# The front of a hybrid decoder block: constants, first row tiles, first weight slab and row loads in another order

## The reference

```python
h = rmsnorm(x, g_mix[l])
proj = h @ w_in[l]          # 1024 x 4000
c_q, c_kv, k_rope_raw, bcx, gate_logits = jnp.split(
    proj, [COL_CQ, COL_CKV, COL_KROPE, COL_CONV], axis=-1)
attn = mla_attention(c_q, c_kv, k_rope_raw, cos, sin, g_cq[l], w_uq[l], g_ckv[l], w_ukv[l])
conv = gated_short_conv(bcx, conv_w[l])
gates = jax.nn.sigmoid((gate_logits + b_gate[l]).astype(jnp.float32)).astype(x.dtype)
mixed = g_a * (attn @ w_branch_a[l]) + g_b * (conv @ w_branch_b[l])
x = x + mixed @ w_out[l]
```

## Time and profile before

| | us |
|---|---|
| median of 3 runs | 2920.02 |
| lowest and highest | 2916.92, 2920.36 |
| the profiled execution | 2914.94 |
| its span in the profile | 2913.1 |
| PE busy in it | 2670.8 (92%) |
| DVE busy | 1669.3 (57%) |
| ACT busy | 1387.2 (48%) |
| POOL busy | 665.4 (23%) |

### The profile page before, as it was taken

One profiled execution on the slowest core, in us unless ns is written; L12 is line 12 of the kernel. 1 busy time (PEld: TensorE's weight loads), 2 busy tenths in 40 slices (PEclk: granted clock), 3 DMA queues, 4 the chain that ended last, 5 costly groups with the idle time before them and its releaser, 6 DMA issues. The chain is left out here.

```text
span 2913.1 us, 37842 instructions
## 1 busy us (share of the span) xinstructions
PE 2670.8 (92%) x12830; PEld 2083.5 (72%) x12830; DVE 1669.3 (57%) x2262; ACT 1387.2 (48%) x2316; POOL 665.4 (23%) x708
## 2 busy tenths in 40 slices
PE   6999999999998999999799999899967999999980
PEld 5777787787775666666689898677656777777760
DVE  3623624524426666655554453465566888888858
ACT  4334334324323666667611112543416777777853
POOL 0000000000003555555322220000003444444420
PEclk9999999999998999999899999999978999999995
DMA  4253353354442112212345344232267999999978
GB/s 167 83 189 130 109 171 115 124 171 169 131 134 48 37 39 55 47 37 75 108 131 150 112 134 160 84 109 102 77 255 267 370 373 374 374 383 387 374 279 353
DMA packets 168851, 508.67 MB, mean 175 GB/s; under 512 B 40448, under 2 KB 69760, under 8 KB 140576
## 3 DMA queue, kind: packets, MB, share of 16 engines
q1 hardware_dynamic: 150016, 472.56, 47.4%
q0 software_dynamic: 18720, 34.64, 3.2%
HBM read 432.21 MB, written 108.33 MB: 186 GB/s over the span
## 5 line engine op out<-in xcount | busy, mean ns | idle before, releaser
L487 DVE TENSOR_TENSOR fr_wl<-fr_raw,fr_wh 128x1024 fp32r<-128x1024 f32 x128 | 156.8, 1225 | 470.5 <-ACT fr_wh L358 470.2
L358 ACT CAST fr_wh<-fr_raw 128x1024 fp32r<-128x1024 f32 x128 | 134.0, 1047 | 493.0 <-PE fr_acc L282 493.0
L2547 DVE TENSOR_TENSOR ex_gl<-ba_raw,ex_gh 128x2048 fp32r<-128x2048 f32 x128 | 293.2, 2292 | 101.8 <-ACT ex_gh L2460 101.8
L2460 ACT CAST ex_gh<-ba_raw 128x2048 fp32r<-128x2048 f32 x128 | 245.2, 1917 | 39.5 <-PEq L2055 39.5
L909 ACT ACTIVATE at_pf<-at_psS 128x512 f32<-128x512 f32 (+1 forms) x320 | 178.3, 558 | 167.1 <-PE at_psS L794 84.2
L1027 POOL TENSOR_TENSOR at_pl<-at_pf,at_ph 128x512 fp32r<-128x512 f32 (+1 forms) x160 | 195.4, 1221 | 258.7 <-ACT at_ph L910 258.2
L983 DVE TENSOR_TENSOR at_pl<-at_pf,at_ph 128x512 fp32r<-128x512 f32 (+2 forms) x160 | 145.7, 914 | 139.7 <-ACT at_ph L910 136.5
L944 DVE TENSOR_REDUCE at_nm<-at_psA 128x1 f32<-128x512 f32 (+2 forms) x320 | 183.0, 605 | 63.2 <-PE at_psA L828 43.1
L2397 PE MATMUL ex_psG<-ex_gh,ex_xh 128*128 128x512 f32 x512 | 200.7, 392 | 6.7 <-DVE ex_xl L2552 5.3
L2398 PE MATMUL ex_psG<-ex_gl,ex_xh 128*128 128x512 f32 x512 | 200.3, 391 | 0.0
L2399 PE MATMUL ex_psG<-ex_gh,ex_xl 128*128 128x512 f32 x512 | 200.1, 391 | 0.0
(11 more groups left out here) (367 smaller groups left out, 6469.7 us busy)
## 6 DMA issues: line engine op xcount, KB each, us to landing
ba_raw<-in_w_exp SPq DMA_DIRECT2D x192, 1024.0 KB, 19.0
fr_raw<-in_w_slabs SPq DMA_DIRECT2D x128, 512.0 KB, 3.8
gates_d<-fr_gst SPq DMA_DIRECT2D x64, 256.0 KB, 4.3
mx_gt<-gates_d SPq DMA_DIRECT2D x64, 256.0 KB, 5.3
cb_ys<-y_d SPq DMA_DIRECT2D x16, 1024.0 KB, 10.9
mx_xr<-in_x SPq DMA_DIRECT2D x8, 1024.0 KB, 7.1
x_d<-mx_xo SPq DMA_DIRECT2D x8, 1024.0 KB, 5.0
xa_xe<-x_d SPq DMA_DIRECT2D x16, 512.0 KB, 5.5
```

The costliest lines, as they stand in the source:

```text
L487: V.tensor_tensor(wl[:, i % 2], raw[:, i % 2], wh[:, i % 2], ALU.subtract).then_inc(w_lo, 1)
L2460: nc.scalar.copy(gh[:, s, i], raw[:, r, i, :].rearrange("p (k n) -> p k n", k=KD // 2)).then_inc(w_hi, 1)
L2547: V.tensor_tensor(gl[:, s, i], raw[:, r, i, :].rearrange("p (k n) -> p k n", k=KD // 2), gh[:, s, i], ALU.subtract).then_inc(w_lo, 1)
```

## The change: what it does

1. **Constants.** The block for `cst`, `vec` and `masks` is gone. Their three loads are issued in the front's SP queue, after tile 1 and ahead of slab 0. PE waits for them ahead of the first turn, ACT and DVE after their part of the start.
2. **Table.** ACT computes one square root of one column (of `eps`) before it waits for tile 0.
3. **Banks.** Tiles 1 and 2 are turned into `psL` 0, 1 and 2, 3; tile 3 goes into `tp` again and waits for tile 0 alone. ACT splits tile 3 ahead of casting slab 1, and DVE splits tiles 2, 3 in another order about the first `low`.
4. **First slab.** Its first eight matmuls wait for the four `hh` and for `wh`, the next eight for `wl`, the last for `hl`.
5. **PE kept busy.** 14 products of `ones` by `ones` (128 x 128, 32-bit) ahead of the first turn, four after each of the four turns. Their result is not used.
6. **Rows.** The first two tiles of quarters 2 and 3, and the two tiles of mem, are issued at n = 26 and 27 of the quarter before the one in which they are turned (that is, 5 or 6 slabs ahead of where they were). The first two tiles of quarter 1 are still issued at n = 0 and 1 of quarter 0. The others stay at n = 4 and 6.

```diff
-                pe.wait_ge(out_lo, ti)
+                if ti >= 4:
+                    pe.wait_ge(out_lo, ti)
+                elif ti == 3:
+                    pe.wait_ge(out_lo, 1)
...
+            for dst, src in zip((cst, vec, masks), consts):
+                sp.dma_start(dst[:], src).then_inc(c_in, 16)
...
-                    if more and n in (0, 1, 4, 6):
-                        rows(TQ * (q + 1) + (0, 1, 4, 6).index(n))
-                    if not more and n < MT:
-                        rows(NT + n)
+                    if q == 0 and n < 2:
+                        rows(TQ + n)
+                    if more and n in (4, 6):
+                        rows(TQ * (q + 1) + n // 2)
+                    if more and n in (26, 27):
+                        rows(TQ * (q + 2) + n - 26)
...
+                if i == 0:
+                    pe.wait_ge(out_hi, 2 * TQ)
+                    pe.wait_ge(w_hi, 1)
...
+                    if i == 0 and j == 1:
+                        pe.wait_ge(w_lo, 1)
+                    if i == 0 and j == 2:
+                        pe.wait_ge(out_lo, TQ)
...
+            pe.wait_ge(ones_set, 1)
+            keep_busy(14)
+            pe.wait_ge(c_in, 48)
             for ti in range(TQ):
                 turn(ti)
+                keep_busy(4)
...
+            nc.scalar.activation(st[:, 3, 1:2], eps[:], ACT.Sqrt)
...
-        with nc.Block() as block:
-            @block.sync
-            def _(sp):
-                sp.dma_start(cst[:], a["consts"]).then_inc(c_in, 16)
-                sp.dma_start(vec[:], a["vecs"]).then_inc(c_in, 16)
-                sp.dma_start(masks[:], a["masks"]).then_inc(c_in, 16)
-                sp.wait_ge(c_in, 48)
```

More of the change, by code:

```diff
@@ L100, in front @@
 def front(nc, cst, vec, x, g_mix, w_slabs, pos, w_uq, w_uk, w_uv, gates_d, conv_d, qn_d, qr_d, kn_d, kr_d, v_d,
-          mem, g_mem, w_kv, hh0, hl0, wk_mem, wv_mem, memT, kv_in):
+          mem, g_mem, w_kv, hh0, hl0, wk_mem, wv_mem, memT, kv_in, masks, consts, c_in):
     QS = 1.0 / math.sqrt(QKD)
@@ L171, in x_landed, with turn_space @@
             return (x_in[ti], 16) if ti < 4 else (x_in[ti % 2], 16 * (2 + (ti - 4) // 2))
+        def turn_space(ti, half):
+            if ti in (1, 2):
+                return psL[2 * (ti - 1) + half][:].rearrange("p (k n) -> p k n", k=4)
+            return tp[half][:]
         def angle_count(q):
@@ L264, in turn, with keep_busy @@
                 pe.wait_ge(norm_done, ti + 1)
-                pe.wait_ge(out_lo, ti)
+                if ti >= 4:
+                    pe.wait_ge(out_lo, ti)
+                elif ti == 3:
+                    pe.wait_ge(out_lo, 1)
                 for k in range(KD):
-                    mm = nc.tensor.transpose(tp[k // 4][:, k % 4, :], xn[:, ti % 2, k * P:(k + 1) * P], ident)
+                    mm = nc.tensor.transpose(turn_space(ti, k // 4)[:, k % 4, :], xn[:, ti % 2, k * P:(k + 1) * P], ident)
                 mm.then_inc(turned, 1)
+            def keep_busy(n):
+                for _ in range(n):
+                    nc.tensor.matmul(acc[1][:, 0:P], ones[:], ones[:], start=True, stop=True)
             def slab(q, n):
                 i = N * q + n
-                if n == 0:
-                    pe.wait_ge(out_lo, TQ * (q + 1))
-                pe.wait_ge(w_lo, i + 1)
+                if i == 0:
+                    pe.wait_ge(out_hi, 2 * TQ)
+                    pe.wait_ge(w_hi, 1)
+                else:
+                    if n == 0:
+                        pe.wait_ge(out_lo, TQ * (q + 1))
+                    pe.wait_ge(w_lo, i + 1)
                 if i >= 2:
@@ L403, in split_out @@
                 for half in (1, 0):
-                    nc.scalar.copy(hh[Q % 2][:, 4 * half:4 * half + 4, tile], tp[half][:]).then_inc(out_hi, 1)
+                    nc.scalar.copy(hh[Q % 2][:, 4 * half:4 * half + 4, tile], turn_space(ti, half)).then_inc(out_hi, 1)
             def memory_out(m):
@@ L450, in _ @@
             split_out(2)
+            split_out(3)
             high(1)
-            split_out(3)
+            act.wait_ge(c_in, 48)
             for q in range(NC_):
@@ L504, in split_out @@
                     f = slice(4 * half, 4 * half + 4)
-                    ins = V.tensor_tensor(hl[Q % 2][:, f, tile], tp[half][:], hh[Q % 2][:, f, tile], ALU.subtract)
+                    ins = V.tensor_tensor(hl[Q % 2][:, f, tile], turn_space(ti, half), hh[Q % 2][:, f, tile], ALU.subtract)
                 ins.then_inc(out_lo, 1)
@@ L602, in _ @@
             norm(3)
+            split_out(2)
             low(0)
-            split_out(2)
+            split_out(3)
             low(1)
-            split_out(3)
+            dve.wait_ge(c_in, 48)
             for q in range(NC_):
@@ L2734, in program @@
             front(nc, cst, vec, x, a["g_mix"], a["w_slabs"], a["positions"], a["w_uq"], a["w_uk"], a["w_uv"], gates_d, conv_d, qn_d, qr_d, kn_d, kr_d, v_d,
[L2735 removed]
+                  a["mem"], a["g_mem"], a["w_kv_mem"], hh0, hl0, wk_mem, wv_mem, memT, kv_in, masks, (a["consts"], a["vecs"], a["masks"]), c_in)
             at = -(-nc.sbuf_base // 32) * 32
```

## The result

| | before | changed |
|---|---|---|
| median, us | 2918.53 (4 runs, 2916.92 to 2920.36) | 2891.03 (4 runs, 2888.50 to 2892.51) |
| ratio | | 0.9906, 95% interval 0.9894 to 0.9919 |
| second comparison | 2915.27 (9 runs) | 2892.42 (5 runs), ratio 0.9923 (0.9909 to 0.9936) |
| profiled execution, its span | 2914.94, 2913.1 | 2891.18, 2889.4 |

The kernel is faster by 27.5 us in the first comparison and by 22.9 in the second. The prediction was 2893.0, with 2886 to 2901.

The account below looks back on a forecast made before the run. PE's waits at the start and where quarters begin, with the low clock after them, were taken to bound the front. 10.8 + 16.2 = 27.0 us off the median 2920.02 gave 2893.0, range 2886 to 2901.

Parts of the forecast that it names:

- The quarters' beginnings: Where quarters 1 to 3 begin: edit 6 removes PE's waits and the low clock after them, 16.2 us (12 to 16.6).
- the 0.5 us of slack: Quarter 1's beginning: next slab's cast, subtraction and norm end at about 243.6; PE wants the turn at 244.1.
- the 0.4 us left for this: Quarters' beginnings: allowance for the late slab load, taken off 16.6; quarter 1 holds, quarter 2 misses by some 0.2 us.
- The sign named for a wrong mechanism: In the changed profile: slab loads showing as releaser of ACT's cast by over 1 us would mean the prediction was wrong.
- The start: Front up to the second slab: edits 1 to 5 bring it forward by 10.8 us (8.5 to 12.5).
- four-us pace: First tiles: each took about 4 us, turn, cast, subtraction, next turn, in a chain; edit 3 lets these pieces overlap.
- warm and cold cases: Slab 0's clock: full, second slab at 25.9, 11.4 us earlier; low until then, at 27.2, 10.1 us earlier.
- less at the start: Tiles 1 to 3 paced by loads and ACT's in-order queue, not banks: start gives 7.8, total 2896.0; chance 0.13.
- the slab in the tile's place: Quarters' beginnings: slab's load late by 1.5 us or more, 12 of 16.6 kept, total 2897; chance 0.10.
- held gate stores: Moved row loads hold up gate stores queued behind them on SP: 11 us given back, total 2904; chance 0.04.
- no effect of the move: Quarters' beginnings: ACT waits for something else, so edit 6 does nothing; the start alone, 2909; chance 0.03.
- the slower case: Front: PE works some 830 us without rest and the chip halves the clock; ten slow slabs make 2947; chance 0.02.

Follow-up runs that it names:

- the second profile: The changed kernel run and profiled again with no further edit: front's end 827.66 us (827.85 in its first profile), median 2892.42 us against 2915.27 before.

## Why the prediction was right, and where it was off

- **The quarters' beginnings**, 16.2 forecast, 16.4 found in the profile and 15 to 16 by time alone. The releaser named in the earlier trace rows was the cause, and what is late next was the slab's load. Its margin was read too wide: against PE, ACT's cast in quarter 1 came 0.8 us later than the prediction's times have it (1.75 us ahead of the last group, not 2.5), so the 0.5 us of slack there was used up and the turn was 0.2 us late. In the second profile the cast is 0.5 us later and the turn just on time. Quarter 2, where 0.2 us was to be lost, lost nothing. So the 0.4 us left for this was enough, but the loss came in another quarter than expected. The sign named for a wrong mechanism, a slab load that releases ACT's cast by over 1 us, was set too tight: ACT's wait for that load is 2.77 us in quarter 1 and 2.17 in quarter 2, and PE loses 0.2 us by it in all.
- **The start**, 10.8 forecast, 11.8 found, inside its bounds. The schedule was right to 0.6 us at PE's marks (DVE's last subtraction, expected to end at 23.5, ended at 22.3), but its parts were not sized right. Undone one at a time, in one profile each, edits 1 and 2, the banks of edit 3 and edit 4 are worth 1.8, 1.8, 1.85 and 1.4 us at the front's end, and edit 5 is worth 3.0. The prediction had made edit 3 the one that lets the pieces overlap; its banks are one part among five, and what its new order of ACT and DVE gives was not measured. The step that failed is that reading of the four-us pace: with the clock up, two banks give a pace of 3.3 us too, as the turn itself had been half of the chain.
- **Edit 5** was undersized: the clock is worth 3.0, where the prediction's warm and cold cases lie 1.3 apart, as PE's slow turns stand on the path, too. That the 14 early products buy nothing was right.
- **Edit 2** was called covered by `gb` up to 0.4 us; it is worth 1.8. Costing it at the first norm alone left out that the same ACT queue has the next three tiles, and that the later first turn met the low clock.
- **Rivals.** By size, less at the start, the slab in the tile's place, held gate stores and no effect of the move did not happen, though the first had the mechanism half right: ACT, in its order, waits for tiles 1 and 2, and the banks are worth less than 2 us. PE worked from 20 to 824 us with no gap but the 0.2 us in quarter 1 and the clock stayed at 1.00, so neither did the slower case.
- **The sum** of 27.0 stands against 28.3 in the front and 22.9 to 27.5 in time. What was missing is not in the front: the stages behind it vary by several us with the low clock at their own idle times. That the forecast of 2893.0 lies only 2.0 us from 2891.03 is in part luck: the front gave 1.3 us more than forecast, the stages behind it gave some back, and the median of before, with a fourth run, came out 1.5 us lower.

## What to carry over

Where an engine works through its queue in order, look at what stands ahead of a load in the issuing queue: a store that waits for the last product held up a load that had nothing to do with it, and moving the load by even a few entries, past that store, gave all of the gain. Each of the six idle times of PE at the quarters' beginnings was followed by slow matmuls, so count these with it, as a range (here 1.6 to 3.2 us) and not as a number. For changes of a few us, compare the time at which a stage ends in the profile; here it repeats to some 0.7 us, where the whole time varies by 4 to 12. To tell effects smaller than that apart takes more than one profile of each kernel.

## What had not been expected of the hardware

After idle times of nearly equal length (2.91 and 2.96 us) at the same place, the clock stayed low for one group of eight matmuls in the kernel before and for nearly two in the one with edits 1 to 5. The first 14 products of ones took 4.9 us in one profile of the changed kernel and 6.0 in the next, so the clock rose at another moment, in the same program. And 131 KB in rows of 1 KB ahead of a 512 KB load, together with a load moved up behind it, made it land 1.7 us later. Of this 0.5 is its later issue and 0.3 their share of the bytes; some 0.9 us is left without a cause shown, in one profile.
